# Head of a hybrid decoder step: gate projections tile by tile, and the last rows stored in halves

## What is computed

```python
def project(x, g_pre, w_in, pos):
    u = rmsnorm(x, g_pre) @ w_in
    q_m, k_m, v_m, o_m, z_m, i_m, f_m, q_n, kvc, kvs, kvw, g_n, z_n = jnp.split(u, cuts, axis=-1)
    gates = jax.nn.sigmoid(g_n)

def mlstm_group(...):
    qk, new_buf = causal_conv(jnp.concatenate([q_m, k_m], axis=-1), conv_buf, w_conv, b_conv)
    ig = i_m + b_igate                       # 4 heads
    fl = jax.nn.log_sigmoid(f_m + b_fgate)   # 4 heads
    h, C, n, m = mlstm_chunked(q, k, v, ig, fl, C0, n0, m0)

def merge(x, h_m, z_m, o_n, z_n, w_out, g_post):
    y = jnp.concatenate([h_m * silu(z_m), o_n * silu(z_n)], axis=-1) @ w_out
    return x + rmsnorm(y, g_post)
```

## Time and profile before

| what | value |
|---|---|
| runs before, us | 1086.70, 1084.59, 1086.29; median 1086.29 |
| profiled execution, its own time | 1080.76 us |
| its span, first to last instruction | 1079.0 us |
| mean granted clock of TensorE | 0.996 |
| PE busy | 1036.1 us (96% of the span) |
| DVE, ACT, POOL busy | 473.4, 335.4, 68.0 us |
| first transposed tile starts | 11.52 us |
| group 0 starts on PE | 41.07 us |
| last store issued | 1075.83 us |

### The profile page before, as it was taken

One profiled execution on the slowest core, in us unless ns is written; L12 is line 12 of the kernel. 1 busy time (PEld: TensorE's weight loads), 2 busy tenths in 40 slices (PEclk: granted clock), 3 DMA queues, 4 the chain that ended last, 5 costly groups with the idle time before them and its releaser, 6 DMA issues.

```text
span 1079.0 us, 14564 instructions
## 1 busy us (share of the span) xinstructions
PE 1036.1 (96%) x5353; PEld 620.3 (57%) x5353; DVE 473.4 (44%) x1041; ACT 335.4 (31%) x816; POOL 68.0 (6%) x173
## 2 busy tenths in 40 slices
PE   4999999999999999999999999999999899999997
PEld 3556664444445555578675555666656688445443
DVE  5454333100112222232345888777766466453542
ACT  5421110000001111111104677667766542122121
POOL 1000000000000001112001010100200410000000
PEclk9999999999999999999999999999999999999999
DMA  9402001030402124163101300000020658533512
GB/s 320 180 2 77 1 7 72 0 100 1 81 0 92 28 40 97 35 122 67 55 1 46 106 7 2 1 2 1 2 79 2 155 168 237 176 118 106 168 47 77
DMA packets 83917, 77.49 MB, mean 72 GB/s; under 512 B 29362, under 2 KB 68446, under 8 KB 83782
## 3 DMA queue, kind: packets, MB, share of 16 engines
q1 hardware_dynamic: 72470, 61.84, 19.0%
q10 hardware_dynamic: 11376, 14.72, 5.4%
HBM read 66.59 MB, written 14.10 MB: 75 GB/s over the span
## 4 chain that ended last, share of the span: by engine, by line
PE 86%; DVE 6%; DMA 2%; ACT 2%; issue 2%; SPq 1%; ACTq 0%; DVEq 0%
PE PS L2140 28%; PE PS L2133 14%; PE PS L2382 9%; PE PS L2196 7%; PE PS L2215 6%; PE PS L2228 6%; PE PS L2069 2%; PE PS L2202 1%; DMA WR<-in_w_out 1%; PE PS L2055 1%; PE PS L2411 1%; DMA out_s_C<-GM 1%; SPq L728 1%; PE PS L2138 1%; PE PS L2097 1%
## 5 line engine op out<-in xcount | busy, mean ns | idle before, releaser
L2140 PE MATMUL PS<-WR,XT 128*128 128x512 f32 (+1 forms) x768 | 306.9, 558 | 0.0
L2140 PEld LDWEIGHTS PS<-WR,XT 128*128 128x128 f32 x768 | 144.4, 191 | 147.3 <-issue 144.2
L2133 PE MATMUL PS<-XT,WR 128*128 128x352 f32 x576 | 173.0, 460 | 2.1 <-ACT QN L1046 2.1
L2133 PEld LDWEIGHTS PS<-XT,WR 128*128 128x128 f32 x576 | 108.7, 191 | 61.0 <-ACT QN L1046 2.6
L1616 DVE TENSOR_REDUCE XT<-PS 128x1 f32<-128x640 f32 (+7 forms) x128 | 84.4, 701 | 27.2 <-PE PS L2202 26.7
L2196 PE MATMUL PS<-KTR,XT 64*128 64x512 f32 (+3 forms) x352 | 79.1, 508 | 0.4 <-ACT XT L1176 0.2
L1176 ACT ACTIVATE XT<-PS,XT 128x640 f32<-128x640 f32 (+7 forms) x96 | 66.7, 701 | 9.0 <-DVE XT L1616 8.8
L2215 PE MATMUL PS<-cst,XT 128*128 128x128 f32 x396 | 61.9, 280 | 4.3 <-DVE XT L1627 3.2
L2382 PE MATMUL PS<-WR,KT 128*128 128x512 f32 x128 | 61.0, 599 | 1.6 <-DMA WR<-in_w_out 1.6
L2382 PE MATMUL PS<-WR,QT 128*128 128x512 f32 x128 | 61.2, 599 | 0.0
L1627 DVE TENSOR_SCALAR XT<-XT,small 128x640 f32<-128x640 f32 (+7 forms) x96 | 53.8, 560 | 3.5
(11 more groups left out here) (471 smaller groups left out, 1212.3 us busy)
## 6 DMA issues: line engine op xcount, KB each, us to landing
WR<-in_w_in SPq DMA_DIRECT2D x24, 512.0 KB, 7.7
WR<-in_cache_kv_cmp SPq DMA_DIRECT2D x56, 128.0 KB, 2.5
MT<-row_factors ACTq DMA_DIRECT2D x16, 256.0 KB, 7.0
WR<-in_w_in SPq DMA_DIRECT2D x32, 128.0 KB, 3.3
QN<-in_cache_kv_win SPq DMA_DIRECT2D x8, 512.0 KB, 5.8
out_y_prompt<-MT ACTq DMA_DIRECT2D x8, 512.0 KB, 2.9
out_s_kv_win<-in_cache_kv_win SPq DMA_DIRECT2D x1, 4064.0 KB
XT<-in_x_prompt ACTq DMA_DIRECT2D x6, 512.0 KB, 4.2
```

Of the source, the lines that this page charges most:

```text
L2133: ins = mm(b[:, 0:THIRD], w[:, k, r // 3 * P:(r // 3 + 1) * P], xt[:, k, r % 3 * THIRD:(r % 3 + 1) * THIRD], **f)
L2140: ins = mm(b[:, 0:width], xt[:, k, r * P:(r + 1) * P], w[:, k, :], **f)
```

## The change

1. **Loads.** SP loads only the identity columns of the constants early; the rest and the page table follow after the rows (semaphore `rest_in`). The five parameter loads move to ACT's queue. The i and f columns of `w_in`, which are neighbours, come in one load of eight columns, so `wmisc` has two loads instead of three; POOL then copies the four f columns to their place (L862 of the changed kernel). The loads of tiles 3 to 8 stand in front of the rest of the constants.
2. **ACT's start.** ACT waits for the epsilon column alone and issues one dummy square root before the first tile's square.
3. **Order on DVE.** The parameters are taken behind the scaling of tile 1; the masks are copied after the last `turn_in`.
4. **PE.** The transposes of tile i are followed by the gate projection of tile i - 1, 128 columns wide (`gate_rows`), instead of two pieces of 512 columns.
5. **Gate chain.** ACT takes the three parts of the first `q_m` row block between the steps of the gate chain (`take_third`).
6. **Tail.** The two sums are added in front of the product with the gain. Of the last row tile the residual is added, and the result stored, in two halves of 512 columns.

```diff
             load_x(0)
-            sp.dma_start(cst[:, :], I["consts"]).then_inc(consts_in, 16)
+            sp.dma_start(ident, I["consts"][:, K_ID:K_ID + P]).then_inc(consts_in, 16)
             load_x(1)
             load_x(2)
-            sp.dma_start(table[:, :].rearrange("o (b n) -> o b n", b=SB), I["page_table"].rearrange("(o b) n -> o b n", o=1)).then_inc(table_in, 16)
-            pr = par_rows
-            sp.dma_start(pr[0:8, :], I["g_pre"].rearrange("l (k p) -> (l k) p", p=P)).then_inc(params_in, 16)
...
-            sp.wait_ge(zeros_ready, 1)
-            for row, c0, width in ((MROW_I, C_I, MH), (MROW_F, C_F, MH), (MROW_G, C_G, 3 * NH)):
+            sp.wait_ge(zeros_ready, 3)
+            for row, c0, width in ((MROW_I, C_I, 2 * MH), (MROW_G, C_G, 3 * NH)):
                 sp.dma_start(wmisc[:, :, row:row + width], w[:, :, c0:c0 + width]).then_inc(wmisc_in, 16)
             for i in range(3, NT + 1):
                 load_x(i)
+            sp.dma_start(cst[:, K_CAUSAL:K_END], I["consts"][:, K_CAUSAL:K_END]).then_inc(rest_in, 16)
+            sp.dma_start(table[:, :].rearrange("o (b n) -> o b n", b=SB), I["page_table"].rearrange("(o b) n -> o b n", o=1)).then_inc(rest_in, 16)
             load_w(0)
             load_w(1)
...
+            pool.wait_ge(wmisc_in, 2 * 16)
+            nc.gpsimd.tensor_copy(wmisc[:, :, MROW_F:MROW_F + MH], wmisc[:, :, MROW_I + MH:MROW_I + 2 * MH]).then_inc(zeros_ready, 1)
...
-            act.wait_ge(zeros_ready, ZEROS)
+            pr = par_rows
+            act.dma_start(pr[0:8, :], I["g_pre"].rearrange("l (k p) -> (l k) p", p=P)).then_inc(params_in, 16)
...
+            act.wait_ge(zeros_ready, 1)
+            link(nc.scalar.activation(xsq[:, 0:1], eps_col, ACT.Sqrt))
             for i in range(NT + 1):
...
+            def take_third(u, third):
+                n = first_tile(u // 4) + 3 * (u % 4)
+                act.wait_ge(proj_done, n + third + 1)
+                b, t = bank(4 + (n + third) % 4), third * THIRD
...
             act.wait_ge(gates_in, 1)
             link(nc.scalar.activation(ge, ge, ACT.Exp))
             nc.scalar.activation(fl, ge, ACT.Ln, bias=1.0).then_inc(gates_exp, 1)
+            take_third(0, 0)
             act.wait_ge(gates_in, 2)
             nc.scalar.activation(g4[64:64 + MH, :], gm_m, ACT.Exp, scale=-1.0)
+            take_third(0, 1)
...
             nc.scalar.activation(dec_rows[0:MH, :], wkc[0:MH, :], ACT.Exp).then_inc(gates_exp, 1)
+            take_third(0, 2)
...
-                act.wait_ge(y_ready, i + 1)
-                act.dma_start(O["y_prompt"][0, i * P:(i + 1) * P, :], yr[:, i % 2, :]).then_inc(y_stored[i % 2], 16)
+                for n, c in enumerate([slice(0, D)] if i + 1 < NT else [slice(0, 512), slice(512, D)]):
+                    act.wait_ge(y_ready, i + 1 + n)
+                    act.dma_start(O["y_prompt"][0, i * P:(i + 1) * P, c], yr[:, i % 2, c]).then_inc(y_stored[i % 2], 16)
...
+                if i == 1:
+                    take_parameters()
                 if i:
                     turn_in(i - 1)
...
+                if half:
+                    s1 = yss[:, i % 2 * 2:i % 2 * 2 + 2]
+                    tt(s1[:, 0:1], s1[:, 0:1], s1[:, 1:2], ALU.add).then_inc(y_sum, 1)
                 c = slice(half * 512, half * 512 + 512)
                 tt(yr[:, i % 2, c], bank(2 + 3 * half), gpost[:, c], ALU.mult).then_inc(y_tmp, 1)
                 if half == 0 and i:
                     finish_rows(i - 1)
-                if half:
-                    s1 = yss[:, i % 2 * 2:i % 2 * 2 + 2]
-                    tt(s1[:, 0:1], s1[:, 0:1], s1[:, 1:2], ALU.add).then_inc(y_sum, 1)
...
-                stt(yr[:, i % 2, :], yr[:, i % 2, :], r, xr[:, i % 2, :], op0=ALU.mult, op1=ALU.add).then_inc(y_ready, 1)
+                for c in [slice(0, D)] if i + 1 < NT else [slice(0, 512), slice(512, D)]:
+                    stt(yr[:, i % 2, c], yr[:, i % 2, c], r, xr[:, i % 2, c], op0=ALU.mult, op1=ALU.add).then_inc(y_ready, 1)
...
+            def gate_rows(i):
+                pe.wait_ge(xt_ready, i + 1)
+                if i == 0:
+                    pe.wait_ge(zeros_ready, ZEROS)
+                for k in range(KC):
+                    ins = mm(bank(4 + i // 4)[:, i % 4 * P:(i % 4 + 1) * P], wmisc[:, k, :], xt[:, k, i * P:(i + 1) * P],
+                             start=k == 0, stop=k == KC - 1)
+                if i % 4 == 3:
+                    ins.then_inc(proj_done, 1)
...
-                if i >= 5:
-                    if i == 5:
-                        pe.wait_ge(wmisc_in, 3 * 16)
-                        pe.wait_ge(xt_ready, NT // 2)
-                    for k in range(2 * (i - 5), 2 * (i - 4)):
-                        ins = mm(bank(4), wmisc[:, k, :], xt[:, k, 0:512], start=k == 0, stop=k == KC - 1)
+                if i == 0:
+                    pe.wait_ge(params_in, 5 * 16)
+                    nc.tensor.transpose(bank(4)[:, 0:48], par_rows[0:48, :], ident[0:48, 0:48]).then_inc(par_turned, 1)
+                else:
+                    gate_rows(i - 1)
```

More of the change, by code:

```diff
@@ L391, in build @@
         consts_in = sem("consts_in")
-        table_in = sem("table_in")
+        rest_in = sem("rest_in")
         params_in = sem("params_in")
@@ L751, in store_state @@
                 sp.dma_start(O["s_C"][:, :, h, :, :].rearrange("l b v k -> v (l b) k"), c_all[h]).then_inc(c_in[h], 16)
-            sp.wait_ge(table_in, 16)
+            sp.wait_ge(rest_in, 2 * 16)
             sp.wait_ge(proj_done, ALL)
@@ L837, in _ @@
             for n in range(2):
-                sp.wait_ge(y_stored[n], NT // 2 * 16)
+                sp.wait_ge(y_stored[n], (NT // 2 + n) * 16)
             sp.wait_ge(outs_done, 10 * 16)
@@ L856, in link @@
                 pool.wait_ge(pool_step, steps[0])
+            nc.gpsimd.memset(eps_col, EPS).then_inc(zeros_ready, 1)
+            nc.gpsimd.memset(lns_col, LNS).then_inc(zeros_ready, 1)
             nc.gpsimd.memset(wmisc, 0.0).then_inc(zeros_ready, 1)
@@ L961, in _ @@
                 sort_sample(b)
-        ZEROS = 7
+        ZEROS = 8
         @block.scalar
@@ L974, in link @@
                 act.wait_ge(act_step, steps[0])
-            act.wait_ge(zeros_ready, ZEROS)
+            pr = par_rows
+            act.dma_start(pr[0:8, :], I["g_pre"].rearrange("l (k p) -> (l k) p", p=P)).then_inc(params_in, 16)
+            act.dma_start(pr[8:40, :], I["w_conv"].rearrange("l j (k p) -> (l j k) p", p=P)).then_inc(params_in, 16)
+            act.dma_start(pr[40:48, :], I["b_conv"].rearrange("l (k p) -> (l k) p", p=P)).then_inc(params_in, 16)
+            act.dma_start(bias_i[0:MH, :], I["b_igate"].rearrange("l h -> h l")).then_inc(params_in, 16)
+            act.dma_start(bias_f[0:MH, :], I["b_fgate"].rearrange("l h -> h l")).then_inc(params_in, 16)
+            act.wait_ge(zeros_ready, 1)
+            link(nc.scalar.activation(xsq[:, 0:1], eps_col, ACT.Sqrt))
             for i in range(NT + 1):
@@ L994, in evac_sample @@
                     .then_inc(evac_act, 1)
+            act.wait_ge(zeros_ready, ZEROS)
             for half in range(2):
@@ L1005, in _ @@
             evac_sample(2, 0)
+            def take_third(u, third):
+                n = first_tile(u // 4) + 3 * (u % 4)
+                act.wait_ge(proj_done, n + third + 1)
+                b, t = bank(4 + (n + third) % 4), third * THIRD
+                w = min(THIRD, T - t)
+                ins = nc.scalar.activation(raw[:, u % 2, 3 + t:3 + t + w], b[:, 0:w], ACT.Copy)
+                if third == 2:
+                    ins = nc.scalar.activation(sqk[:, u, :], b[:, w:THIRD], ACT.Copy)
+                ins.then_inc(evac_act, 1)
             act.wait_ge(gates_in, 1)
@@ L1037, in _ @@
             for u in range(8):
-                n = first_tile(u // 4) + 3 * (u % 4)
                 if u >= 2:
                     act.wait_ge(conv_done, u - 1)
[L1042 to L1049, removed]
+                if u:
+                    for third in range(3):
+                        take_third(u, third)
                 if u >= 1:
@@ L1341, in link, with take_parameters @@
                 dve.wait_ge(dve_step, steps[0])
[L1343 to L1347, removed]
+            def take_parameters():
+                dve.wait_ge(par_turned, 1)
+                link(nc.vector.tensor_copy(par, bank(4)[:, 0:48]))
+                link(nc.vector.tensor_scalar(par[:, 8:48], par[:, 8:48], 0.5, None, op0=ALU.mult))
             def turn_in(i):
@@ L1367, in _ @@
             turn_in(NT)
+            dve.wait_ge(rest_in, 2 * 16)
+            dve.wait_ge(consts_in, 16)
+            nc.vector.tensor_copy(masks[:, :], cst[:, 0:K_MT]).then_inc(masks_ready, 1)
             dve.wait_ge(evac_act, 2)
@@ L1935, in _ @@
             pe.wait_ge(consts_in, 16)
-            pe.wait_ge(params_in, 5 * 16)
-            nc.tensor.transpose(bank(4)[:, 0:48], par_rows[0:48, :], ident[0:48, 0:48]).then_inc(par_turned, 1)
+            def gate_rows(i):
```

(13 more changed lines are left out.)

7 lines of the change are left out of this document (removed).

## The result

| | before | changed kernel |
|---|---|---|
| runs, us | 1086.70, 1084.59, 1086.29, 1080.80 | 1074.71, 1071.77, 1069.95, 1071.87 |
| median, us | 1085.44 | 1071.82 |
| profiled execution: its time, span, granted clock | 1080.76, 1079.0, 0.996 | 1074.71, 1072.9, 0.992 |

The ratio of the runs on record is 0.9898, with a 95% interval of 0.9879 to 0.9917. Taken on 1085 us that is 11.1 us less, 9.0 to 13.1; the two medians of four runs lie further apart, 13.6 us. The forecast was 10.3 us less, 1076.0, in a range from 1072 to 1081.5. The forecast gain lies in the interval; the median itself is 0.2 us under the range.

A forecast was written before the change was run, and what follows sets the result against it. PE, busy 1036.1 of 1079.0 us, was taken to set the time. Gains of 7.5 (head), 2.1 (stall) and 0.7 (tail) sum to 10.3 us: 1086.3 - 10.3 = 1076.0 us, range 1072 to 1081.5.

The forecast's parts named there:

- Step 1: Head: PE's first transposes start at about 6.96 us instead of 11.52, 4.56 us earlier.
- Step 2: Head: the first gate matmul starts at 11.05 us, behind `turn_in` of tile 0, with its loads already there.
- landing of the gate weights: Head loads: gate weights land at 8.9 us, 9.2 with POOL's copy, 1.8 us before the first gate matmul.
- Step 3: Head: PE alone sets the pace from 11.05 us; group 0 starts at 33.55 instead of 41.07, 7.5 us gained.
- the rival of weight loads as the pace: In `gate_rows`: load and matmul one behind the other take 299 ns a pair, kernel slower, 1100.0 us; chance 0.04.
- the slow start: Head: first eight transposes take 1.98 us against 0.87 later; part of the first gate tile still slow, 0.5 us.
- main term: Head: gate tiles of 1.79 us each, 14.3 us for eight, within the 7.5 us gained before group 0.
- Step 4: Group 0, at 60.27 us: PE's stall behind ACT's evacuations goes entirely, 2.1 us gained.
- Step 5: Tail behind the last matmul: last store issued 0.15 us sooner and 0.55 us shorter, 0.7 us gained.
- Downstream: Behind the head: a clock-bound transfer ends as late as before, PE waits some 9 us more, 1085 us; chance 0.04.

## Why the prediction was right, step by step

- **Step 1, start of the transposes, 6.96 forecast:** 6.95 measured, 7.03 to 7.14 in three other executions of the same head. The price of the two table loads, checked by leaving the dummy out, is 2.7 us there. Moving the parameters out of the way was not undone by itself, so its share of the 4.6 us is argued from the earlier trace rows and not shown.
- **Step 2, first gate matmul at 11.05:** 12.3 in the timeline of the first profile, 11.1, 11.2 and 11.8 in three others of the same head. What was wrong is that tile 1 was assumed to be there in time. It landed between 6.3 and 8.0. On DVE `turn_in` of tile 0 stands behind the scaling of tile 1, and so waits for it: in the first profile tile 1 is squared at 8.03 and scaled at 9.74, and `turn_in` comes at 10.86. PE idles and the half rate lasts longer. Tile 3 was wrong too, forecast near 9.8 and taken by ACT at 12.41 and 10.75, since its issue was held for 3.5 to 5.0 us behind the narrow loads; but PE never waited for it. The forecast's landing of the gate weights, 9.2 with POOL's copy, was 9.2 and 10.6.
- **Step 3, group 0 at 33.55:** the price of the short gate matmuls was exact, 1.79 us a tile, so the rival of weight loads as the pace fell, and with it the ratio that the Trainium skill gives (TensorE: Matmul & The Clock Gate, Back-to-back issue gap): the trace does not agree with it for float32, 4 x 112 against 430 ns. What was undersized is the slow start, put at 0.5 us in the first gate tile; it cost 0.5 to 1.4. The forecast named a gate tile of over 3 us as the sign that its main term was wrong. In two of four executions the first tile took 3.2 us, but no later one did, and the main term held. Starts of 36.0, 35.5, 34.2 and 34.0 in four executions have a mean of 34.9, 1.4 us later than forecast.
- **Step 4, the stall, 2.1:** gone entirely, 1.9 to 2.1, and it comes back alone when the interleaving is undone. Tile 3 of group 0 was read by 42.67, 12.6 us before it was needed; the forecast had 12.4.
- **Step 5, the tail, 0.7:** 0.9. The last store is issued 3.05 us after the last square instead of 3.36, so 0.3 sooner where 0.15 was forecast, and from there to the end it is 0.6 less, where 0.55 was.
- **Missing in the forecast:** that the old head itself is not one number. In one of three executions it started group 0 1.6 us late, with a fall of the clock. With group 0 at 41.07, 41.0 and 42.6 before, mean 41.6, the parts are 6.7 + 2.0 + 0.9 = 9.6 us, inside the intervals of the two measurements (9.0 to 13.1 and 9.5 to 14.1), at their lower ends.
- **The rest is clock, and partly luck:** the runs of the changed kernel had a mean clock of 0.9943 (9 runs), those of the kernel before 0.9917 (54 runs), which is 2.0 us by the slope. Their mean times lie 11.4 us apart, and 9.4 are left, close to the 9.6 of the parts. So the sum came out well partly by luck: the head gave 0.8 us less than its 7.5, and the clock, which the forecast left out, gave more than that back. Whether the change itself makes the clock higher stays open; with the dummy root left out it was 0.9906. The forecast's time was too high by 4.2 us also because it started from a median of 1086.3, where the medians of the kernel before were 1083.2 to 1085.4 in all that followed.
- **Downstream:** no new wait. What moves between executions is the wait for the output weights, 0.5 to 4.8 us, and the dips of the clock.

## What to carry to other kernels

Where one engine feeds PE piece by piece and PE waits between the pieces, cut the next work on PE as finely as the pieces come; in float32 four matmul instructions of 128 columns took 448 ns here and one of 512 took 430, so next to nothing is paid for it. Read a fixed stall by what its releaser still has in front of it, and move the short reading up, not the long chain down. In a kernel whose executions spread over 0.5%, judge a gain of 1 to 2 us by milestones in several profiles and not by one span against another, and set the mean granted clocks beside the times before a microsecond is put down to the edit.

## What was not expected of the hardware

- PE's first work ran at half rate (eight transposes 1.94 us long, the next eight 1.97, then 1.04), while the granted clock in the rows read 1.00 from the start; later falls of the clock do show in it (0.57 and 0.66). With PE busy on zeros from 2.70 us on, the first eight took 1.11. The Trainium skill, page TensorE: Matmul & The Clock Gate, Part 1, says that an idle array starts at 1.2 GHz and gets 2.4 once it has been busy; these lengths agree. The row of the changed kernel over its first transposes, columns as in the earlier trace rows:

```profile
7.00:9.00 2.00, 2.00 (x9) 1.67 (x9) 0.00 (x0) 0.97 (x2) 0.00 (x0) 1.00 0.70 144
```

- A load of 4 KB rows behind two loads of 32 and 96 bytes a piece was held for 3.5 to 5.0 us at its issue, on a queue where it takes 0.45 otherwise.
- One and the same row tile was taken by ACT at 6.26 to 8.03 us in four executions with the same loads in the same order.
- Between head and tail, PE's stall and its wait for the output weights left out, the time of 13 executions of eleven kernels follows the granted clock within 0.8 us: 0.76 us for each us that it fell short.
